# Low weight halves of the down projections made by accumulating transfers instead of VectorE subtractions

## The reference

```
mix = concat([attn_out, ssd_out]) @ w_out                # 1536 -> 1024
h   = layer_norm(ALPHA * h + mix)
gate, val = split(h @ w_up, 2)                           # 1024 -> 2 x 2816
gate = depthwise_conv(gate, ffn_conv_w, ffn_conv_b)      # width 3
ffn  = (silu(gate) * val) @ w_down                       # 2816 -> 1024: the down projection
h    = layer_norm(ALPHA * h + ffn)
```

## Time and profile before

| | us |
|---|---|
| time, median of 2 runs (1308.72 to 1309.05) | 1308.88 |
| time of the profiled execution | 1309.08 |
| its span, first to last instruction | 1307.3 |
| PE busy | 1296.5 |
| DVE busy | 805.2 |
| ACT busy | 581.1 |
| POOL busy | 96.7 |

### The profile page before, as it was taken

The page is one execution under the profiler, slowest core; times in us unless marked ns, Lnnn a source line. Parts: engine busy times, 40 slices in busy tenths (PEclk is TensorE's granted clock), DMA queues, the critical chain, the costliest instruction groups (busy, mean ns, idle before and its releaser), DMA issues.

```text
span 1307.3 us, 16441 instructions
## 1 busy us (share of the span) xinstructions
PE 1296.5 (99%) x6720; PEld 1071.7 (82%) x6720; DVE 805.2 (62%) x1093; ACT 581.1 (44%) x877; POOL 96.7 (7%) x87
## 2 busy tenths in 40 slices
PE   8999999999999999999999999999999999999997
PEld 8877778889888888888898777788888888888886
DVE  7888789866444444342378987888654444443425
ACT  5766655436333333311276665444453333332112
POOL 2013400001000000000020333000000000000000
PEclk9999999999999999999999999999999999999999
DMA  5421212513333333433143212133223333334332
GB/s 187 160 70 60 61 59 65 180 63 123 98 99 95 99 98 96 130 98 97 54 130 133 65 50 81 51 142 115 81 97 97 97 97 97 97 98 130 97 97 111
DMA packets 33786, 129.17 MB, mean 99 GB/s; under 512 B 3792, under 2 KB 4208, under 8 KB 32560
## 3 DMA queue, kind: packets, MB, share of 16 engines
q1 hardware_dynamic: 33552, 127.84, 30.7%
q0 software_dynamic: 160, 0.29, 0.1%
HBM read 121.82 MB, written 6.29 MB: 98 GB/s over the span
## 4 chain that ended last, share of the span: by engine, by line
PE 97%; DVE 2%; DMA 0%; ACT 0%; issue 0%; DVEq 0%
PE ps L841 18%; PE ps L843 18%; PE ps L842 18%; PE ps L978 9%; PE ps L979 9%; PE ps L980 9%; PE ps L867 4%; PE ps L1194 2%; PE ps L1208 1%; PE ps L1218 1%; PE ps L1228 1%; PE ps L970 1%; PE ps L1168 1%; PE ps L1129 1%; PE ps L1178 1%; PE ps L1137 1%
## 5 line engine op out<-in xcount | busy, mean ns | idle before, releaser
L841 PE MATMUL ps<-hhi,whi 128*128 128x512 f32 x1040 | 407.7, 392 | 0.0
L843 PE MATMUL ps<-hhi,wlo 128*128 128x512 f32 x1040 | 405.0, 389 | 0.0
L842 PE MATMUL ps<-hlo,whi 128*128 128x512 f32 x1040 | 404.9, 389 | 0.0
L1286 DVE TENSOR_TENSOR wlo<-raw,whi 128x1024 fp32r<-128x1024 f32 x208 | 254.1, 1223 | 151.5 <-ACT whi L591 151.5
L591 ACT ACTIVATE whi<-raw 128x1024 fp32r<-128x1024 f32 x208 | 219.3, 1056 | 219.5 <-DMA raw<-in_units 219.5
L841 PEld LDWEIGHTS ps<-hhi,whi 128*128 128x128 f32 x1040 | 195.2, 188 | 41.2 <-issue 1.0
L843 PEld LDWEIGHTS ps<-hhi,wlo 128*128 128x128 f32 x1040 | 195.2, 188 | 41.0
L842 PEld LDWEIGHTS ps<-hlo,whi 128*128 128x128 f32 x1040 | 195.3, 188 | 40.3
L978 PE MATMUL ps<-whi,uhi 128*128 128x512 f32 x352 | 137.1, 390 | 0.0
L980 PE MATMUL ps<-wlo,uhi 128*128 128x512 f32 x352 | 137.0, 389 | 0.0
L979 PE MATMUL ps<-whi,ulo 128*128 128x512 f32 x352 | 136.9, 389 | 0.0
(11 more groups left out here) (185 smaller groups left out, 1480.7 us busy)
## 6 DMA issues: line engine op xcount, KB each, us to landing
raw<-in_units SPq DMA_DIRECT2D x208, 512.0 KB, 3.6
gb<-in_gb SPq DMA_DIRECT2D x5, 1024.0 KB, 5.6
h_kept<-hb SPq DMA_DIRECT2D x2, 2048.0 KB, 9.0
ha<-h_kept SPq DMA_DIRECT2D x2, 2048.0 KB, 8.2
hb<-in_x SPq DMA_DIRECT2D x4, 512.0 KB, 5.9
out_y<-hb SPq DMA_DIRECT2D x8, 256.0 KB, 2.0
cn<-in_cn SPq DMA_DIRECT2D x1, 599.5 KB, 10.2
raw<-in_units SPq DMA_DIRECT2D x2, 128.0 KB, 3.4
```

The costliest lines, as they stand in the source:

```text
L841: mm(out, whi[:, slot, cols], xhi, start=start, stop=False)
L842: mm(out, whi[:, slot, cols], xlo, start=False, stop=False)
L843: return mm(out, wlo[:, slot, cols], xhi, start=False, stop=stop)
L1286: V.tensor_tensor(wlo[:, m % RING, :], raw[:, m % RING, :], f(whi[:, m % RING, :]), ALU.subtract).then_inc(unit_split, 1)
```

## The change

For the 22 down units of each layer, and for these alone, the low part is made in another way. After its copy into `whi`, ACT also writes the negative of it over the loaded values (`wlo = -whi`), and counts `low_minus`. POOL waits for `low_minus` and issues a transfer that reads the unit from memory a second time and adds it onto `wlo` (`accum_op`), so that `wlo` becomes value minus high part; it has a semaphore of its own for each slot (`low_added`). DVE leaves these units out. PE waits for `low_added` where it waited for `unit_split`. All other units are as before, with `unit_split` counted over them alone.

```
+        low_minus = sem("low_minus")
+        low_added = [sem(f"low_added{k}") for k in range(RING)]
...
+        def by_dma(m):
+            return m % UNITS >= U_DOWN
...
+        def wait_split(eng, m):
+            if by_dma(m):
+                eng.wait_ge(low_added[m % RING], 16 * sum(by_dma(n) and n % RING == m % RING for n in range(m + 1)))
+            else:
+                eng.wait_ge(unit_split, splits(m + 1))
...                                             # POOL, behind lows(2 * L + 1)
+                for n in range(U_DOWN, UNITS):
+                    m = unit(L, n)
+                    pool.wait_ge(low_minus, adds(m + 1))
+                    pool.dma_start(wlo[:, m % RING, :], units[m], accum_op=ALU.add).then_inc(low_added[m % RING], 16)
...                                             # ACT, split(m)
+                    if by_dma(m):
+                        act.wait_ge(unit_hi, m + 1)
+                        A(wlo[:, m % RING, :], f(whi[:, m % RING, :]), ACT.Copy, scale=-1.0).then_inc(low_minus, 1)
...                                             # PE, down projection
-                    pe.wait_ge(unit_split, unit(L, U_DOWN + k) + 1)
+                    wait_split(pe, unit(L, U_DOWN + k))
...
-                    pe.wait_ge(unit_split, unit(L, UNITS))
+                    for n in range(UNITS - LAST, UNITS):
+                        wait_split(pe, unit(L, n))
...                                             # PE, final_units
-                                pe.wait_ge(unit_split, used + j + 1)
+                                wait_split(pe, used + j)
...                                             # DVE, split(m)
-                if m < DEPTH * UNITS:
+                if m < DEPTH * UNITS and not by_dma(m):
```

More of the change, by code:

```diff
@@ L415, in unit, with splits, adds @@
             return L * UNITS + n
+        def by_dma(m):
+            return m % UNITS >= U_DOWN
+        def splits(m):
+            return sum(not by_dma(n) for n in range(m))
+        def adds(m):
+            return sum(by_dma(n) for n in range(m))
+        def wait_split(eng, m):
[3 more added lines that the diff above has]
+                eng.wait_ge(unit_split, splits(m + 1))
         def wait_high(eng, idx, s, j):
@@ L931, in first_units @@
                 split_units = range(idx % 2 == 0, 2)
-                pe.wait_ge(unit_split, used + 1)
+                wait_split(pe, used)
                 for j in range(2):
@@ L936, in first_units @@
                         part(idx, used, 0, 0, kind, (2 * j, 2 * j + 1))
-                pe.wait_ge(unit_split, used + 2)
+                wait_split(pe, used + 1)
                 for kind in ("hi hi", "hi lo"):
@@ L950, in first_units @@
                 transposes(idx, 3)
-                pe.wait_ge(unit_split, used + 3)
+                wait_split(pe, used + 2)
                 for kind in ("hi hi", "hi lo", "lo hi"):
@@ L1055, in _ @@
                             pe.wait_ge(zs_done, L * CT + i - 2 - U_Z + 1)
-                        pe.wait_ge(unit_split, L * UNITS + i + 1)
+                        wait_split(pe, unit(L, i))
                         by_columns(unit(L, i) % RING, unit_bank(i))
@@ L1071, in _ @@
                     elif what == "GT":
-                        pe.wait_ge(unit_split, unit(L, U_UP))
+                        wait_split(pe, unit(L, U_UP) - 1)
                         pe.wait_ge(sl_done, L * CT + CT)
@@ L1079, in _ @@
                         u, banks = i
-                        pe.wait_ge(unit_split, L * UNITS + u + 1)
+                        wait_split(pe, unit(L, u))
                         if u == U_OUT and 2 in banks:
@@ L1247, in _ @@
                         n = U_UP + 2 * k + half
-                        pe.wait_ge(unit_split, unit(L, n) + 1)
+                        wait_split(pe, unit(L, n))
                         by_columns(unit(L, n) % RING, PAIR_BANK[k % 4] + half)
```

## The result

The changed kernel took 1320.52 us (median of 2, 1319.2 to 1321.84) against 1308.88, ratio 1.0089 with a 95% interval of 1.0073 to 1.0105: 11.6 us slower, within 2%. The forecast was 1315. It was the slower of the two by 2.6 us, so the 11.6 us between the medians are known to some 2 us, by the interval.

What follows compares the result with a forecast made beforehand. The prediction took PE to bound the kernel, busy for all but 11 us. Zero for the middle and ACT's copies, 0.7 us at layer 0's end and 5.6 at layer 1's gave 6.3 us, so 1315 us; range 1309 to 1336.

Steps and rivals of the forecast that it cites:

- What bounds the kernel, and the relief of DVE: Whole run: PE bounds it; 54 us off DVE gain nothing; over 2% faster by this had a chance under 0.01.
- Latency and engine time in the middle: Mid down stage: 11.2 us chain within 21.8, slack 10.6; DMA engines need 5.0 of 5.44 us a unit; no cost.
- k = 2: Down stage: an add takes the DMA engine time of two loads, 3.3 us, giving 5.0 of 5.44 us per unit.
- The copies on ACT in the up projection: Last two up-projection blocks: negative copies make silu 0.5 us late, the next load's following operation not late; hidden, cost 0.
- X, the landing: Time from POOL's issue of an add to its landing: 5.3 us, bounded by 3.6 and 11.4.
- End of layer 0: Last down unit of layer 0: POOL issues at 634.9, landing at 640.2, PE waits 0.7 us (0 to 6.8).
- End of layer 1: Last down unit of layer 1: issue at 1280.8, landing at 1286.1, PE waits 5.6 us (2.3 to 11.7).
- The clock: End of layer 1: a PE wait of the forecast length costs no granted clock; size 0.
- Quick adds: Rival: adds as quick as loads, leaving only 2.3 us at layer 1's end or less: 1309 to 1312 us, chance 0.13.
- DMA-bound: Rival, mid down stage: DMA engines become the bound; 1347 us at three loads per add, 1420 at four; chance 0.19.
- Adds slow one by one but overlapping: Rival: landings of 12 to 16 us, hidden mid-stage, naked at layer ends: 1328 to 1336 us, chance 0.06.
- Adds that hold POOL: Rival: issue takes as long as the add; same as the sum while under 5.44 us; counted with slow but overlapping adds.

Runs made afterwards that it cites:

- the plain transfer: Changed kernel with POOL's transfers copying the unit onto the low part instead of adding it, which alters the result: 1312.04 us, ratio 1.0026.
- the run with layer 0 alone: Changed kernel with adds only for the 22 down units of layer 0, layer 1 as before the change: 1311.04 us, ratio 1.0021.
- the kernel with two copies more: Kernel with the last four units of each layer split by DVE, plus two 512 KB memory-to-memory transfers per middle add: 1338.88 us, ratio 1.0233.
- One copy more: Kernel with the last four units of each layer split by DVE, plus one 512 KB memory-to-memory transfer per middle add: 1309.03 us, ratio 1.0002.
- the gains' early load: Changed kernel with the 1 MB load of the last gains issued before the fifth unit from the end's load: 1318.68 us, ratio 1.0075.

## Why the prediction was right, and where its sizes were off

*What bounds the kernel, and the relief of DVE.* Right. 53 us off DVE bought nothing; with 36 adds in the middle, which took their splits off DVE too, the time was 1.0001 of before.

*Latency and engine time in the middle.* Right, and the most valuable of the steps. Load and add together took 4.55 us of all engines for a unit (3.10 and 1.45), where the sum had 5.0 as an upper reading, and the add took 2.1 loads where k = 2 was taken; the plain transfer showed that this is the add's doing (3.1 us against 1.5). The second read stream is the natural reason, and the reduce-scatter rule of the Trainium skill's "Collectives: The Full Stack", under the bandwidth ceiling and the fold count, fits its number, but no run told it from a slow adder of the same price. The slack held where it was used: landings of 11.9 us were hidden, landings with a median of 13.2 were not. By the sum, with the load at 3.6 us, up to 15.9 would have been; the term left out is that a crowd makes the load itself late, 9.7 us in that kernel.

*The copies on ACT in the up projection.* Cost 0, as said: PE was busy for all of the 20 us from 525 to 545. Silu was 0.35 us late in the first of the two blocks of layer 0 (522.94 for 522.59) and 0.34 in the second (533.81 for 533.47), where 0.5 was forecast. That no later operation of a block is late didn't hold for the second: the load came later beside the adds (its copy at 536.62 for 534.76), and the high part `uhi` behind it at 538.68 for 537.26. It stayed covered.

*X, the landing.* Sized at 5.3 us, which is the least that was seen and nearly what an add takes alone (5.5). In the stage it was 6.5 in the median. The term left out is that adds and loads delay each other; I had counted such a crowd only at the end of layer 1. The plain transfer from POOL landed in 3.5 us at the least and 4.6 in the median, above the 3.2 of the estimate for it in the prediction.

*End of layer 0.* 0.7 forecast, 1.9 measured in the trace and 2.1 in the run with layer 0 alone. POOL's issue was at 635.99 instead of 634.9, as the load landed 0.9 us later beside the earlier adds and POOL took 0.3 us to wake.

*End of layer 1.* 5.6 us forecast, 7.2 waited. The last copy came at 1280.76 - 1.94 = 1278.8, where 1278.5 was forecast. That is luck in part: the 1.6 us for the crowding of that load had no working behind it. The last add was issued at 1281.3 for 1280.8 and landed in 7.3 us for 5.3, together 2.5 us later than forecast. The add before it, which the forecast had on time, was issued 1.5 us later than the 1273.9 forecast (1277.30 - 1.94 = 1275.4) and landed in 9.4 us, beside the last load and the gains; but the last one ended last and set the time.

*The clock.* This step was wrong. "A wait of this length costs no clock that I can see" rested on a window at the start in which PE had gaps at full clock. The longest of them was 1.8 us, the longest wait of PE in the whole trace of before (us in total, times, longest):

```profile
PE ps L1031 <- DVE hb L1346: 1.8, 1, 1.8
```

The wait forecast was 5.6 us, three times as long. The trace of the changed kernel has 3.6 us of slow matmuls behind the waits, and the kernel of before, made to wait once for 3.9 us, paid another 2.3. Single waits of up to 2.9 us (in the kernel with two copies more) were followed by no such stretch. It is the largest part of the miss: of 12.7 - 6.3 = 6.4 us, 2.9 are slow matmuls behind the last wait, 2.3 the later arrival at the last unit of layer 1 (7.9 us for 5.6) and 1.2 the wait of layer 0 (1.9 for 0.7). The stated range took the result in because its upper end allowed an X of 11.4, which never came, and not because it had this term.

*The rivals.* Quick adds: ruled out by landings never under 5.3 us. DMA-bound: it didn't happen in this change but was made to happen with two more copies; its sum was too pessimistic. Two copies more make 7.55 us a unit by the shares, 2.11 over the pace, at which its formula for 18 units a layer gives 2 x (18 x 2.11 - 10.6) = 55 us, and the run lost 30. One copy more, at 6.05 us, lies below the 6.4 of k = 2.8; the formula gives 1 us there, and nothing was lost. Adds slow one by one but overlapping: X wasn't 12 to 16, but the mechanism, hidden in the middle and naked at the ends, is what happened at 6.5. Adds that hold POOL: ruled out, an issue took 0.86 us.

What stays open: how the 3.1 us of an add divide between reading the destination and adding, how much of the gains' early load reaches the median, and what makes the clock fall behind one pair of short waits and not behind another.

## What to carry to other kernels

Before giving an idle queue a longer way to the same buffer, read the slack at the ends of the stage, where several buffers are wanted at once, and not in its middle: here 10 us of slack in the middle hid 36 adds, and 1.3 us at the very end did not hide one. Leave the last few on the short way, or use first what is ready first. Price a wait of a bound TensorE at more than its length once it is some 4 us long, or when shorter ones stand close together.

## What the runs showed of the hardware

- An accumulating 512 KB transfer took 3.1 us of all DMA engines against 1.5 for the same transfer without the add, landed in 5.3 us at the least against 3.5, and its issue took 0.86 us on POOL against 0.53.
- TensorE ran at 1.2 GHz behind waits of 3.9 us and more, with matmuls of 512 columns starting 0.43 us apart, for 12 matmuls behind a wait of 3.9 us, for eight behind one of 4.8, and for some 10 us behind waits of 4.8 and 2.4. Behind 26 single waits of up to 2.9 us, with a unit's 24 matmuls between them, they went on at 0.23.
- Two shorter waits with two or three matmuls between them could bring the low clock as well: eight slow matmuls after waits of 0.88 and 1.83 us, seven after 1.66 and 2.76 (the gains loaded earlier), none after 0.66 and 1.62 (the plain transfer).
- A DMA share of 1.02 in the profile was still no bound: the stage ran at full pace at 296 GB/s. With one copy more for each unit the share was 1.01 and the rate 323 GB/s, and the stage was slower. Engine times summed from shares of quieter stretches gave 7.55 us for a unit that took 6.2.
